# Three widths for the second slot of an expert, with its columns in strips of eight rows

## The reference

```python
logits = (h @ w_router).astype(jnp.float32)
top_v, top_i = lax.top_k(logits, TOP_K)            # TOP_K = 2
top_w = jax.nn.softmax(top_v, axis=-1)
combine = jnp.sum(jax.nn.one_hot(top_i, N_EXPERTS) * top_w[..., None], axis=-2)
for e in range(N_EXPERTS):                         # 8
    out = out + combine[..., e:e + 1] * swiglu(h, w_gate[e], w_up[e], w_down[e])
# swiglu: (silu(h @ w_gate) * (h @ w_up)) @ w_down, w_gate and w_up 1024x1408, w_down 1408x1024
```

## Time and profile before

| | before |
|---|---|
| time, median of 3 runs | 1551.89 us (1551.81 to 1552.09) |
| span of the profiled execution, first to last instruction | 1550.1 us |
| PE busy | 1529.5 us, 99% of the span |
| DVE, ACT, POOL busy | 71%, 56%, 22% |
| first expert matmul | 1051.06 us |
| expert sections 0 and 1 (two slots) | 1051.06 to 1195.68 us |
| expert sections 2 to 5 (one slot) | 1195.68 to 1389.22 us |
| expert sections 6 and 7 (two slots) | 1389.22 to about 1531 us |
| granted TensorE clock, mean | 0.998 |

### The profile page before, as it was taken

One profiled execution on the slowest core, in us unless ns is written; L12 is line 12 of the kernel. 1 busy time (PEld: TensorE's weight loads), 2 busy tenths in 40 slices (PEclk: granted clock), 3 DMA queues, 4 the chain that ended last, 5 costly groups with the idle time before them and its releaser, 6 DMA issues.

```text
span 1550.1 us, 24600 instructions
## 1 busy us (share of the span) xinstructions
PE 1529.5 (99%) x8392; PEld 1321.4 (85%) x8393; DVE 1099.5 (71%) x1784; ACT 872.2 (56%) x1418; POOL 333.7 (22%) x350
## 2 busy tenths in 40 slices
PE   8999999999999999999999999999999999999997
PEld 6888888888999988887888888879898888889895
DVE  7657765758989963436657766776676998887587
ACT  5436665335445442224347764565576888886564
POOL 0204564003544600002015662010000011110000
PEclk9999999999999999999999999999999999999999
DMA  6732212242453233336322112519777999997773
GB/s 221 205 99 69 64 66 82 83 149 84 161 182 131 89 123 91 98 105 153 108 78 80 59 63 88 190 65 327 254 254 256 364 383 373 391 376 267 239 257 132
DMA packets 89793, 265.79 MB, mean 171 GB/s; under 512 B 12497, under 2 KB 22737, under 8 KB 89680
## 3 DMA queue, kind: packets, MB, share of 16 engines
q1 hardware_dynamic: 82864, 248.59, 47.0%
q0 software_dynamic: 6816, 15.74, 3.5%
HBM read 242.84 MB, written 19.83 MB: 169 GB/s over the span
## 4 chain that ended last, share of the span: by engine, by line
PE 93%; DVE 3%; ACT 1%; DMA 1%; issue 1%; SPq 0%; DVEq 0%; ACTq 0%; POOLq 0%
PE ps L1978 14%; PE ps L1983 14%; PE ps L1979 14%; PE ps L2384 8%; PE ps L2359 5%; PE ps L2361 5%; PE ps L2360 5%; PE ps L2386 3%; PE ps L2264 2%; PE ps L2265 2%; PE ps L2272 2%; PE ps L2145 2%; PE ps L2233 2%; PE ps L2234 2%; PE ps L2238 2%; PE ps L2178 1%
## 5 line engine op out<-in xcount | busy, mean ns | idle before, releaser
L973 ACT ACTIVATE w_hi<-raw 128x1024 fp32r<-128x1024 f32 (+1 forms) x124 | 129.3, 1043 | 214.2 <-PE ps L1983 211.1
L1978 PE MATMUL ps<-h_hi,w_hi 128*128 128x512 f32 x544 | 219.9, 404 | 1.0 <-DVE h_lo L1395 0.6
L1979 PE MATMUL ps<-h_lo,w_hi 128*128 128x512 f32 x544 | 212.9, 391 | 0.0
L1983 PE MATMUL ps<-h_hi,w_lo 128*128 128x512 f32 x544 | 212.7, 391 | 0.0
L1375 DVE TENSOR_TENSOR m_lo<-m_raw,m_hi 128x1024 fp32r<-128x1024 f32 x144 | 167.9, 1191 | 58.8 <-ACT m_hi L1016 50.9
L1370 DVE TENSOR_TENSOR w_lo<-raw,w_hi 128x1024 fp32r<-128x1024 f32 (+1 forms) x94 | 112.9, 1201 | 101.6 <-ACT w_hi L973 96.7
L1016 ACT ACTIVATE m_hi<-m_raw 128x1024 fp32r<-128x1024 f32 x144 | 145.3, 1031 | 54.2 <-PE ps L2358 25.9
L2384 PE MATMUL ps<-xt,m_hi 128*128 128x320 f32 x592 | 154.3, 347 | 0.3 <-issue 0.3
L2386 PE MATMUL ps<-xt,m_lo 128*128 128x160 f32 x592 | 140.3, 237 | 0.0
L1983 PEld LDWEIGHTS ps<-h_hi,w_lo 128*128 128x128 f32 x544 | 102.1, 188 | 22.4
L1375 DVE TENSOR_TENSOR m_lo<-h_rows,m_hi 128x1024 fp32r<-128x1024 f32 (+1 forms) x96 | 102.0, 1087 | 22.1 <-ACT m_hi L1016 21.7
(11 more groups left out here) (371 smaller groups left out, 4066.9 us busy)
## 6 DMA issues: line engine op xcount, KB each, us to landing
m_raw<-moe_g SPq DMA_DIRECT2D x88, 512.0 KB, 5.4
raw<-w_in SPq DMA_DIRECT2D x68, 512.0 KB, 3.3
m_raw<-moe_down SPq DMA_DIRECT2D x56, 512.0 KB, 5.7
raw<-w_gu SPq DMA_DIRECT2D x44, 512.0 KB, 3.9
h_rows<-moe_g SPq DMA_DIRECT2D x32, 512.0 KB, 5.1
h_rows<-moe_g SPq DMA_DIRECT2D x32, 384.0 KB, 4.7
h_rows<-moe_down SPq DMA_DIRECT2D x24, 512.0 KB, 5.6
m_raw<-moe_g SPq DMA_DIRECT2D x24, 384.0 KB, 5.4
```

Of the source, the lines that this page charges most:

```text
L973: A.activation(split_of(n, 0, cols)[0], raw[:, n % RAW, 0:cols], ACT.Copy).then_inc(hi_ready, 1)
L1978: E.matmul(ps[:, bank, :], wh, hi, start=first, stop=False)
L1979: E.matmul(ps[:, bank, :], wh, lo, start=False, stop=False)
L1983: return E.matmul(ps[:, bank, :], wl, hi, start=False, stop=final)
```

## The change

The second slot's columns no longer stand in one piece of 32. `xt` (and PSUM) hold low of slot 0 in columns 0 to 127, high of slot 0 in 128 to 255, and then strips of 8 rows of slot 1: 8 high, 8 low, 8 high, 8 low, and so on up to column 319. So the first 8, 16 or 32 rows of slot 1, high and low, are a contiguous run with slot 0. TensorE's `one_pass` takes a `width` of 8, 16 or 32, by the count (up to 136, 144, 160 rows):

- L2384's successor sends `2 * P + 2 * width` columns: 272, 288 or 320;
- L2386's successor sends columns 128 to `run - 8`: 136, 152 or 184;
- each of the three places (first, loop, last) has three two-slot bodies and one one-slot body. The order in the program is: a compare with 128 (false goes to the one-slot body), with 136, with 144; the 32-wide body; the 8-wide body; the 16-wide body; the one-slot body; the end.

ACT and DVE still move all 32 rows, now through four-dimensional views of strips, and DVE's addition is two instructions (slot 1's 32 rows, slot 0's 128) where it was one of 160.

```diff
+STRIP = 8
+WIDTHS = (8, 16, TAIL)
...
+        def x_slot0(part):
+            return slice((1 - part) * P, (2 - part) * P)
+        def strips(of, part):
+            return of[:, :, 2 * P:2 * P + 2 * TAIL].rearrange("p k (q i r) -> p k q i r", i=2, r=STRIP)[:, :, :, part, :]
...
                 def low_columns(which, bank, nb):
-                    A.activation(m_other[:, which, 0:nb, 0:TAIL], ps[:, bank:bank + nb, CAP + P:2 * CAP], ACT.Copy)
-                    A.activation(m_other[:, which, 0:nb, TAIL:CAP], ps[:, bank:bank + nb, CAP:CAP + P], ACT.Copy).then_inc(tail_moved, 1)
+                    A.activation(in_strips(m_other[:, which, 0:nb, P:CAP]), strips(ps[:, bank:bank + nb, :], 1), ACT.Copy)
+                    A.activation(m_other[:, which, 0:nb, 0:P], ps[:, bank:bank + nb, x_slot0(1)], ACT.Copy).then_inc(tail_moved, 1)
...
+            def both_parts(out, bank, which, nb):
+                V.tensor_tensor(in_strips(out[:, 0:nb, P:CAP]), strips(ps[:, bank:bank + nb, :], 0), in_strips(m_other[:, which, 0:nb, P:CAP]), ALU.add)
+                return V.tensor_tensor(out[:, 0:nb, 0:P], ps[:, bank:bank + nb, x_slot0(0)], m_other[:, which, 0:nb, 0:P], ALU.add)
...
-            def one_pass(i, first, slots, turn_next=True, opening=False):
+            def one_pass(i, first, slots, turn_next=True, opening=False, width=TAIL):
+                run = 2 * P + 2 * width
...
-                            E.matmul(ps[:, bank + b, 0:2 * CAP], hi_of(u)[:, at:at + P], xt[:, k, P - TAIL:3 * P + TAIL],
-                                     start=k == 0, stop=False)
-                            mm = E.matmul(ps[:, bank + b, 0:CAP], lo_part(u)[:, at:at + P], xt[:, k, P - TAIL:2 * P], start=False, stop=k == KD - 1)
+                            E.matmul(ps[:, bank + b, 0:run], hi_of(u)[:, at:at + P], xt[:, k, 0:run], start=k == 0, stop=False)
+                            mm = E.matmul(ps[:, bank + b, P:run - STRIP], lo_part(u)[:, at:at + P], xt[:, k, P:run - STRIP],
+                                          start=False, stop=k == KD - 1)
...
+            def sections(name, rows, some_pass):
+                E.br_cond(rows > P, on_true=f"{name}_over{P}", on_false=f"{name}_one")
+                for j, width in enumerate(WIDTHS):
+                    with nc.body(f"{name}_over{P + (WIDTHS[j - 1] if j else 0)}", valid_engines=[E.engine]):
+                        if j < len(WIDTHS) - 1:
+                            E.br_cond(rows > P + width, on_true=f"{name}_over{P + width}", on_false=f"{name}_{width}")
+                        else:
+                            ahead = E.mark_branch_hint_location()
+                            some_pass(SLOTS, width)
+                            E.br(f"{name}_end").branch_hint(ahead)
+                for width in WIDTHS[:-1]:
+                    with nc.body(f"{name}_{width}", valid_engines=[E.engine]):
+                        ahead = E.mark_branch_hint_location()
+                        some_pass(SLOTS, width)
+                        E.br(f"{name}_end").branch_hint(ahead)
+                with nc.body(f"{name}_one", valid_engines=[E.engine]):
+                    some_pass(1, TAIL)
+                    E.br(f"{name}_end")
```

More of the change, by code:

```diff
@@ L373, in slot_columns, with x_part @@
         def slot_columns(sl):
[L374 to L379, removed]
+            return slice(0, P) if sl == 0 else slice(P, CAP)
+        def x_slot0(part):
+            return slice((1 - part) * P, (2 - part) * P)
+        def strips(of, part):
+            return of[:, :, 2 * P:2 * P + 2 * TAIL].rearrange("p k (q i r) -> p k q i r", i=2, r=STRIP)[:, :, :, part, :]
+        def x_part(part, sl, k0, k1):
+            return strips(xt[:, k0:k1, :], part) if sl else xt[:, k0:k1, x_slot0(part)]
         def at_parts(sl, c0, c1):
@@ L387, in used_columns, with in_strips @@
         def used_columns(of, sl):
-            return of if sl == 0 else of[:, :, 0:TAIL]
+            return of if sl == 0 else in_strips(of[:, :, 0:TAIL])
+        def in_strips(of):
+            return of.rearrange("p k (q r) -> p k q r", r=STRIP)
         def step(s):
@@ L1816, in turned_x @@
                     V.wait_ge(xt_hi_ready, done + (2 * sl + hb + 1))
-                    hi, lo = (xt[:, 4 * hb:4 * hb + 4, x_part(part, sl)] for part in range(2))
+                    hi, lo = (x_part(part, sl, 4 * hb, 4 * hb + 4) for part in range(2))
                     lo_of(lo, used_columns(ps[:, banks[sl] + hb, :].rearrange("p (k c) -> p k c", c=P), sl), hi).then_inc(xt_lo_ready, 1)
@@ L2373, in token_products @@
                     for k in (2 * j, 2 * j + 1):
-                        mm = products(ps[:, 0 if what == "gate" else 2, 0:w], xt[:, :, x_part(0, 0)], xt[:, :, x_part(1, 0)], None, 0, k,
+                        mm = products(ps[:, 0 if what == "gate" else 2, 0:w], xt[:, :, x_slot0(0)], xt[:, :, x_slot0(1)], None, 0, k,
                                       u, (k % 2) * w, w, k == 0, k == KD - 1)
@@ L2453, in one_pass @@
                             turn_rows(TURN_X.index(u), i * 16 + 16 * (first + 2))
[L2455 to L2462, removed]
@@ L2463, in _ @@
[L2463 to L2473 removed]
+            def sections(name, rows, some_pass):
[16 more added lines that the diff above has]
+                    E.br(f"{name}_end")
+                nc.switch_bb(f"{name}_end")
@@ L2475, in place_last, with rows_of @@
+            def rows_of(p):
+                return E.value_load(counts[0:1, p], min_val=0, max_val=T)
+            sections("first", rows_of(slice(0, 1)), lambda slots, width: one_pass(0, 0, slots, opening=True, width=width))
+            with nc.Fori(0, LAST - 1, engines=[E.engine]) as i:
+                sections("next", rows_of(bass.ds(i + 1, 1)), lambda slots, width: one_pass(i, 1, slots, width=width))
             def place_last(slots):
@@ L2488, in place_last, with last_pass @@
                         mm.then_inc(placed, 1)
-            with E.If(E.value_load(counts[0:1, LAST:N_SEC], min_val=0, max_val=T) > P):
-                one_pass(0, LAST, SLOTS, turn_next=False)
-                place_last(SLOTS)
-            with E.Else():
-                one_pass(0, LAST, 1, turn_next=False)
-                place_last(1)
+            def last_pass(slots, width):
+                one_pass(0, LAST, slots, turn_next=False, width=width)
+                place_last(slots)
+            sections("last", rows_of(slice(LAST, N_SEC)), last_pass)
             with E.If(E.value_load(most[0:1, 0:1], min_val=0, max_val=T) > CAP):
```

16 lines of the change are left out of this document (3 added, 13 removed).

## The result

The changed kernel takes 1557.88 us (median of 4 runs, 1555.59 to 1561.21), the kernel before on the same chip 1551.85 (4 runs). The ratio is 1.0044, 95% interval 1.0032 to 1.0056: slower, by 6 us. The forecast was 1549.5 us, with a range up to 1554.5.

A forecast was written before the change was run, and what follows sets the result against it. TensorE was taken to bound the kernel: 1550.1 us profiled, less 11.7 for matmuls and 0.4 given back, plus 9.8 for branches, makes 1547.8; with 1.8 to the median, 1549.5 us. Range 1543.5 to 1554.5.

The forecast's parts named there:

- The gain: Gate and up matmuls: 20.0 ns a pair 8 wide, 13.3 ns 16 wide, over 352 pairs each, together 11.7 us.
- its floor: Low-weight matmul: sits on a floor of about 110 ns, the weight load before it, so fewer columns give 0.
- rival 4: Gate and up: the low-weight matmul is shortened too, 4.7 us less, 1544.8 us; chance 0.07.
- ACT and DVE: Two-slot sections: split additions at 284 and 681 ns, 3.4 us more DVE work, hidden; ACT's strips have the same elements.
- Which branches fetch: Sections 0, 1, 2 (back edge and jump), 6 and 7 fetch, 9.8 us together; sections 3 to 5 cost 0.
- Rivals 2 and 3: Branches: rival 2, they cost nothing, 1540.2 us, chance 0.08; rival 3, nothing kept across far jumps, 1567 us, chance 0.10.
- rival 1: Loop's start or 16-wide body's first block at hand: 3.4 and 1.25 us less, take 1546 us; chance 0.15.
- For the fetch I take 3.6 us, a little under the shorter of the two: Each far branch: fetch priced at 3.6 us from two unhinted branches of 3757 and 4214 ns at the kernel's end.
- small waits: Section 2: its stall gives back 0.3 to 0.5 us of PE's waits in small pieces for splits.
- the queue's cover: At the branches: matmuls already queued hide 2.5 to 2.9 us of a fetch in sections 1, 2, 6 and 7.
- The clock: Section 2: about 5 us with an idle array may cost between 0 and 1.5 us of clock; 0.4 taken.
- The exit: End of the last section: two unhinted branches come after the last matmul was queued and cost nothing there.

The follow-up runs named there:

- the run with full columns: The changed kernel with its three bodies and all branches, but every body's matmuls over the full 320 and 184 columns: 1570.7 us, ratio 1.0123.
- the strips and one width: The changed kernel with one width of 16 columns, strips and split additions kept, forms for 8 and over 144 rows left out: 1541.38 us, ratio 0.9934.
- narrow body first: The changed kernel with its bodies in the order 8, 16, 32 columns: 1553.7 us (10 runs), ratio 1.0013.
- the kernel with two widths: The changed kernel without its body for 32 rows, widths 8 and 16 only: 1557.46 us, ratio 1.0039.

## Why the prediction was wrong

- **The gain** held: 12.0 us against 11.7, and 12.8 by the run with full columns. The 8-wide pair gave 20 ns, just what its high-weight matmul was to give, and a low-weight matmul of 184 columns cost no more than one of 160: it did sit on its floor, and rival 4 is out.
- **ACT and DVE** held: with the strips and one width there is no wait for either. The two additions take 292 and 680 ns, where 284 and 681 were forecast.
- **Which branches fetch** held in five of six: sections 0, 1, 2 (twice) and 7 fetched, sections 3 to 5 did not. Section 6's did not either (363 ns): 1.25 us too many. Rivals 2 and 3 are out, and the half of rival 1 that concerns section 6 was true.
- **The step that failed is "For the fetch I take 3.6 us, a little under the shorter of the two".** The five records are 4.3, 4.9, 5.9, 5.4 and 4.7 us, mean 5.0. I took the price from two branches at the kernel's end, where the weight loads are nearly over (91 GB/s from 1535 to 1544 us, against 262 from 1190 to 1200), and then a little less; the four later ones average 5.2, and with the traffic taken away they average 4.25. Stalls, clock and small waits come to 17.2 us in the profiled execution, where 9.8 - 0.4 = 9.4 were forecast. Of the 7.8 us between them, five fetches by 1.4 us are 7.2; the clock adds 1.1, section 6 takes 1.25 off, and 0.9 is left for the queue's cover, which I had a little too long.
- **The reason I gave for 3.6 us failed too.** I judged a fetch by its packets, which were a little shorter in the loop (1.1 us) than at the end (1.3). But the packets are only a part of the fetch. From 1190 to 1206 us in the changed kernel, where the two records of section 2 take 5.9 and 5.4 us, the queue brought five:

```profile
q8 instruction: 5, 0.08, 3.0%
```

That is 3.0% of 16 x 16 us / 5 = 1.5 us each. It would have been wiser to take the dearer row and add for the traffic, since every fetch in question meets weight loads.

- **The clock** was sized too small: "between 0 and 1.5 us, and I take 0.4". It is 1.5 in the profiled execution, and the changed kernel's runs differ by 5.6 us with a mean clock from 0.997 down to 0.992. The small waits of section 2 gave back 0.5 us, as forecast (0.4).
- **The exit** was left out ("cost nothing there"); it gave back 0.9 to 1.0 us, at the edge of what can be told.
- A slip of the sum: 1547.8 and 1.8 are 1549.6 us, not 1549.5.

On the memory of the sequencer the trace and the Trainium skill (Runtime: NRT & Kernel Launch, "Instruction fetch mechanics") differ. The section has the window filled in sequence and a taken branch fetch when its target is outside it. By that, the back edge over 1821 rows with the narrow body first should have fetched; it took 229 ns, and in the changed kernel sections 3 to 5 jump over three bodies and back in 208 to 232 ns. Blocks far apart are kept side by side. The measurement decides. By which rule a block is dropped is open: "last used is kept, about eight" seems to fit most records (no run tested it by itself), but not the second fetch of the one-slot body in section 3, nor the lost start in the kernel with two widths.

## What to carry to other kernels

A gain per instruction that is bought with more copies of a loop's body must be set against the code fetches: count the branches on the path whose target didn't run lately, price each at the dearest fetch seen under the same traffic (here 4.3 to 5.9 us, less 2 to 3 us of queue), and add for the clock behind the stall. Keep the loop as short as it was, let the common case fall through, and put the extra copy where it is passed once. Together with a limit of 144 rows that turned +6 us into -11.5; of the kernels that still serve 160 rows in these sections the best is at -3.3. A wait that a page puts down to a split or to "issue" at a section's start is read together with the sequencer's branch records before anything is done about the split.

## What the runs showed of the hardware

- A branch to code that is not at hand takes 3.7 to 7.2 us, in 30 records in front of the sections of the changed kernel and these runs; one at hand 65 to 449 ns; a hinted jump 184 to 475 ns. The jump out of the last section took 3757 ns without a hint and 322 with one. A hint 70 us ahead with another behind it did nothing (5752 ns).
- A body that is fallen into streams its code in behind the execution without a stall of PE: with the narrow body first the records at sections 0 and 1 are 67 to 71 ns, and the first matmul of section 1 follows in 0.23 us.
- Behind gaps of the array of 1.6 to 9 us the granted clock went to 0.50 for 3 to 10 us, and not behind every such gap: in the changed kernel's profiled execution behind section 2's 8.7 us but not behind those of 2.3 to 2.6 us, in the run with full columns behind section 7's 2.2 us too. Work at 0.50 took twice its time: gate and up of a one-slot section, 31.07 us at the full clock, took 32.58 with 2.9 us of work at 0.50 (changed kernel, section 2) and 34.07 with 6.2 us (narrow body first, section 2). The kernels without a fetch in front of a section read a mean of 0.997 to 0.999, but for one run of the kernel before at 0.996 (1554.31 us).
